# Expert products of a routed mixture: weights loaded in runs of rows, and eight of twelve products a tile as three float32r products each

## Chip, cores and metric

The kernel runs on one core of a Trainium2 chip. The metric is the device time of one execution in microseconds (us). "Before" is the median of three executions.

## What is computed

The program is a whole small model: one mixing block with a hierarchical mixture of experts, then two further layers. Only the mixture matters here. Each of 1024 tokens chooses 2 of 16 experts; an expert is a gated product of width 256.

```
eid = g_idx[:, None] * EXPERTS_PER_GROUP + top_i
gates = jnp.sum(jax.nn.one_hot(eid, N_EXPERTS, dtype=jnp.float32) * weights[..., None], axis=1)
y = jnp.zeros_like(t)                                   # t: 1024 x 1024
for e in range(N_EXPERTS):                              # w_gate, w_up: 1024 x 256, w_down: 256 x 1024
    act = jax.nn.silu(t @ w_gate[e]) * (t @ w_up[e]) * gates[:, e:e + 1]
    y = y + act @ w_down[e]
```

All of it is float32.

## The kernel before

Every engine has its own program, written out by hand; semaphores order them. The mixture is worked in 31 tiles (`MTILES`) of 128 token rows of one expert. Which expert a tile has, its token rows and their weights are tables made on the chip (`et_i`, `tabs`). 2048 rows are filled in, so late tiles are mostly or wholly padding; every tile costs TensorE the same. `experts(eng, step)` (line 583) runs `step(i, o)` for tiles 0 to 2, then a loop of two tiles a turn, then the last four tiles and one step more to drain.

One tile on TensorE, as `expert_pe` (line 1606) orders it:

- `gate_up` (line 1579): the tile's 128 rows stand transposed in `hgT` as eight blocks of 128x128. Each is the stationary operand of one product with 512 columns (256 of w_gate, 256 of w_up), summed in PSUM bank 2 or 3. Eight products, the first five ahead of `turn_act`, three behind it.
- `turn_act` (line 1590): two 128x128 transposes of the previous tile's activations.
- `turn_rows` (line 1571): eight 128x128 transposes of the next tile's gathered rows `hg`.
- `down` (line 1597): the previous tile's two blocks of activations against two halves of w_down: four products of 512 columns.

So a tile has twelve products of 128x128 by 128x512. In float32 each leaves two MATMUL records in the trace. The other engines:

- ScalarE, `expert_act` (line 1133): copies the turned activations out of PSUM (line 1139), the Silu of the gate half (1143), copies the 128x1024 result out of PSUM (1147).
- VectorE, `expert_dve`: gate times up times weight (line 2135), then `rows_to_ht` (line 2122): the turned rows times the norm's gain into `hgT`, two operations of 512 columns (2128).
- SyncE: `load_gu` (line 705) loads w_gate and w_up of tile o+2 once `gate_up` of tile o is done; `load_d` (line 711) loads w_down of tile o+1 once `down` of tile o-1 is done. Weights have two buffers. A partition takes rows p, p+128, ... of a weight matrix, so a run in HBM is one row: 1 KB for gate and up, 4 KB for down.
- GpSimd: `gather` brings the rows of tile o+3, `scatter` writes the result of tile o-1, both as indirect DMAs.

In most of its other large products the kernel already has a split form (`accumulate_split`, line 99): an operand x is kept as hi, a ScalarE copy of x into float32r, and lo = x - hi, a VectorE subtraction; x·w is then hi·hi + hi·lo + lo·hi, three float32r products, each of which leaves one MATMUL record.

Of the kernel before, what the change touches and what calls it, by code (L numbers as in the profile page):

```python
# [46 lines left out]
V_AG, V_FG, V_CB, V_LG, V_LB, V_PB, V_PS, V_QG, V_KG, V_SG, V_CW = 0, 8, 16, 18, 20, 22, 24, 26, 27, 28, 29  # L47
# [63 lines left out]
def program(nc, A, out):  # L111
    ctx = ExitStack()
    with ctx:  # L113
# [6 lines left out]
        def sems(name, n):  # L120
# [42 lines left out]
                    nc.alloc_sbuf_tensor_at("W1c_hi", [P, 2, HALF], F32R, offset=X_at + 4 * 5 * S))  # L163
        lr_rows = nc.alloc_sbuf_tensor_at("LR", [P, S], F32R, offset=WT_at + 4 * S)
# [115 lines left out]
        actT = X[:, M0 + 1024:M0 + 1536].rearrange("p (b k n) -> p b k n", b=2, k=2)  # L280
# [102 lines left out]
        xn_st = sems("xn_st", 2)  # L383
        rw_zero, rw_in, rt_ready, rt_cp, rt_tp = (
# [244 lines left out]
        def _(sp):  # L629
# [75 lines left out]
            def load_gu(i, o):  # L705
                e, p = expert(i, o), o % 2
                wait_past(sp, m_gu, i * 2 + (o - 1))
                sp.dma_start(WT[:, p, :, 0:DE], A["w_gate"][0, ds(e, 1)].rearrange("a (k p) c -> p (a k) c", p=P)).then_inc(m_wgu[p], 16)
                sp.dma_start(WT[:, p, :, DE:2 * DE], A["w_up"][0, ds(e, 1)].rearrange("a (k p) c -> p (a k) c", p=P)).then_inc(m_wgu[p], 16)

            def load_d(i, o):
                e, p = expert(i, o), o % 2
                wait_past(sp, m_dn, i * 2 + (o - 1))
                sp.dma_start(wd[:, p, :, :], A["w_down"][0, ds(e, 1)].rearrange("a (k p) c -> p (a k) c", p=P)).then_inc(m_wd[p], 16)
# [283 lines left out]
        def _(act):  # L998
# [413 lines left out]
        def _(pe):  # L1412
# [158 lines left out]
            def turn_rows(i, o):  # L1571
# [3 lines left out]
                for c in range(KD):  # L1575
                    tp = pe.transpose(bank(c // 4, P, (c % 4) * P), hg[:, p, c * P:(c + 1) * P], ident[:, :])
                tp.then_inc(m_xt, 1)

            def gate_up(i, o, ks):
                p = o % 2  # L1580
                if 0 in ks:
# [833 lines left out]
```

## Time and profile before

| | |
|---|---|
| median of three runs | 2575.41 us (2574.57 to 2576.43) |
| the profiled execution's own time | 2580.86 us |
| its span, first to last instruction | 2579.1 us |
| mean granted TensorE clock | 0.958 of 2.4 GHz |
| busy share: TensorE, VectorE, ScalarE, GpSimd | 91%, 49%, 39%, 18% |
| expert tiles on TensorE | 643.6 to 1002.1 us |
| HBM read, written | 212.13 MB, 41.42 MB |

TensorE's matmul records overlap, since a matmul's end lies behind the start of the next; what a product costs in a stream is the distance between starts, not its duration. All times below are of the profiled execution. It is 0.2% longer than the median of the runs.

### The profile page before, as it was taken

Reading aid. Unit: us, or ns where it says so; the run is one execution under the profiler, and the core shown is the slowest. Engines: PE = TensorE matmul, PEld = TensorE weight load, DVE = VectorE, ACT = ScalarE, POOL = GpSimd, SP = SyncE. Lnnn points to the kernel's source line nnn. Section 1 sums busy time; section 2 is a strip of 40 time slices with the busy share of each in tenths; the row PEclk is TensorE's granted clock in tenths of the full one; section 3 lists DMA queues with packets and bytes.
Section 4 is the critical chain, followed back from the end, with each engine's and each line's share of the span. In section 5 each row is a group of like instructions: output and inputs, shape, how many; then the busy total and the mean of one; then the engine's idle time right before and its main releaser. Section 6 shows DMA issues by size and latency. Waiting matters only on the chain. (4 is left out here: it accounts for less than half of the span.)

```text
span 2579.1 us, 31377 instructions
## 1 busy us (share of the span) xinstructions
PE 2337.2 (91%) x11004; PEld 1758.5 (68%) x11004; DVE 1272.3 (49%) x2049; ACT 1006.3 (39%) x1623; POOL 456.3 (18%) x494
## 2 busy tenths in 40 slices
PE   7999677898999996799999997998899999998996
PEld 5777354684444443677787886887677877886885
DVE  4178777424111113476615776353466426775344
ACT  5222366322111112556453345144566353444233
POOL 1047233210122221311130000000311230000000
PEclk9999889899999997799999999999899999999998
DMA  6200200014899988211110003012111110003021
GB/s 192 94 33 1 93 38 1 9 56 158 282 351 334 328 283 291 95 33 33 34 52 21 11 33 131 33 49 99 35 34 34 33 43 21 11 34 131 33 68 72
DMA packets 207788, 239.71 MB, mean 93 GB/s; under 512 B 45088, under 2 KB 165152, under 8 KB 207648
## 3 DMA queue, kind: packets, MB, share of 16 engines
q1 hardware_dynamic: 197680, 221.06, 25.9%
q0 software_dynamic: 8928, 16.80, 1.8%
q8 instruction: 85, 1.39, 0.2%
q14 instruction: 55, 0.45, 0.1%
q10 hardware_dynamic: 1040, 0.00, 0.0%
HBM read 212.13 MB, written 41.42 MB: 98 GB/s over the span
## 5 line engine op out<-in xcount | busy, mean ns | idle before, releaser
L106 PE MATMUL ps<-WT_lo,HT_hi 128*128 128x512 f32 x832 | 327.5, 394 | 0.0
L107 PE MATMUL ps<-HT_hi,WF_lo 128*128 128x512 f32 x800 | 315.0, 394 | 0.0
L105 PE MATMUL ps<-HT_hi,WU_hi 128*128 128x512 f32 x704 | 285.8, 406 | 18.7 <-DVE H_lo L2169 14.7
L106 PE MATMUL ps<-H_lo,WU_hi 128*128 128x512 f32 x704 | 277.3, 394 | 0.0
L1586 PE MATMUL ps<-WT,MIX 128*128 128x512 f32 x496 | 225.9, 599 | 4.8 <-DVE MIX L2128 4.8
L105 PE MATMUL ps<-W_hi,HT_hi 128*128 128x512 f32 x512 | 204.6, 400 | 8.8 <-DVE MIX_lo L2315 5.9
L107 PE MATMUL ps<-W_hi,MIX_lo 128*128 128x512 f32 x512 | 201.6, 394 | 0.0
L947 POOL TENSOR_TENSOR WF_lo<-WF,WU_hi 128x1024 fp32r<-128x1024 f32 x44 | 115.0, 2614 | 467.8 <-ACT WU_hi L1174 467.8
L106 PEld LDWEIGHTS ps<-WT_lo,HT_hi 128*128 128x128 f32 x832 | 158.8, 191 | 31.8
L107 PEld LDWEIGHTS ps<-HT_hi,WF_lo 128*128 128x128 f32 x800 | 152.4, 191 | 32.9
L105 PEld LDWEIGHTS ps<-HT_hi,WU_hi 128*128 128x128 f32 x704 | 134.3, 191 | 52.0 <-DVE H_lo L2169 15.5
L1586 PEld LDWEIGHTS ps<-WT,MIX 128*128 128x128 f32 x496 | 92.8, 192 | 110.3 <-issue 105.0
L2135 DVE SCALAR_TENSOR_TENSOR X<-X,ps 128x256 f32<-128x256 f32 x31 | 14.9, 481 | 299.8 <-ACT X L1143 299.8
L1349 ACT ACTIVATE xn<-ps,sm 128x1024 f32<-128x1024 f32 x64 | 71.4, 1116 | 222.0 <-DVE sm L2331 222.0
L106 PEld LDWEIGHTS ps<-H_lo,WU_hi 128*128 128x128 f32 x704 | 134.4, 191 | 29.9 <-issue 2.9
L457 POOL TENSOR_SCALAR ss<-ss 128x1 f32<-128x1 f32 x56 | 14.5, 260 | 724.2 <-ACT ps L445 526.0
L445 ACT ACTIVATE ps<-H 128x1024 f32<-128x1024 f32 x40 | 41.1, 1028 | 222.5 <-DVE H L2357 128.6
L464 PE MATMUL ps<-ident,xn 128*128 128x128 f32 x440 | 69.7, 310 | 55.8 <-ACT xn L451 44.7
L105 PEld LDWEIGHTS ps<-W_hi,HT_hi 128*128 128x128 f32 x512 | 97.7, 191 | 29.6 <-DVE MIX_lo L2315 6.3
L95 PE MATMUL ps<-MIX,X 128*128 128x512 f32 x248 | 111.7, 593 | 1.2 <-ACT X L1139 1.2
L107 PEld LDWEIGHTS ps<-W_hi,MIX_lo 128*128 128x128 f32 x512 | 97.6, 191 | 20.9
L464 PEld LDWEIGHTS ps<-ident,xn 128*128 128x128 f32 x440 | 59.3, 160 | 69.2 <-ACT xn L451 50.0
(431 smaller groups left out, 5001.2 us busy)
## 6 DMA issues: line engine op xcount, KB each, us to landing
WT<-in_w_gate SPq DMA_DIRECT2D x31, 1024.0 KB, 5.7
WT<-in_w_up SPq DMA_DIRECT2D x31, 1024.0 KB, 9.2
MIX<-in_w_down SPq DMA_DIRECT2D x31, 1024.0 KB
WF<-in_w_in SPq DMA_DIRECT2D x48, 512.0 KB, 3.8
WT<-in_w_out SPq DMA_DIRECT2D x6, 2048.0 KB, 8.0
H<-in_x SPq DMA_DIRECT2D x16, 512.0 KB, 9.0
h_dram<-H SPq DMA_DIRECT2D x16, 512.0 KB, 3.0
H<-h_dram SPq DMA_DIRECT2D x16, 512.0 KB, 10.7
```

The source lines that it names most:

```text
L95: mm = pe.matmul(o, l, r, start=(i == 0), stop=(i == last))
L105: pe.matmul(o, lh, rh, start=(i == 0), stop=False)
L106: pe.matmul(o, lh, rl, start=False, stop=False)
L107: mm = pe.matmul(o, ll, rh, start=False, stop=(i == last))
L445: act.activation(xn[:, t % 2, :] if squares is None else squares, H[:, t, :], ACT.Square, accum_out=ss[:, t:t + 1]).then_inc(n_ss, 1)
L457: chain.link(pool.tensor_scalar(ss[:, t:t + 1], ss[:, t:t + 1], 1.0 / D, EPS, ALU.mult, ALU.add))
L464: tp = pe.transpose(bank(2 + 2 * (t % 2) + c // 4, P, (c % 4) * P), xn[:, t % 2, c * P:(c + 1) * P], ident[:, :])
L947: pool.tensor_tensor(WFr[:, w, :, 0:n], WF[:, w, :, 0:n], wu_hi[:, w, :, 0:n].bitcast(F32), ALU.subtract).then_inc(ul_ready, 1)
L1349: act.activation(xn[:, g % 2, :], psf[:, (2 + 2 * (g % 2)) * HALF:(4 + 2 * (g % 2)) * HALF], ACT.Exp, scale=MLA_SCALE, bias=sm[:, g % 2, 1 ...
L1586: mm = pe.matmul(bank(2 + p), hgT[:, p, k, :], WT[:, p, k, :], start=(k == 0), stop=(k == KD - 1))
L2135: dve.scalar_tensor_tensor(out=actb[:, o % 2, :], in0=sgb[:, o % 2, :], scalar=tabs_f[:, ds(i * 2 + o, 1), 2:3].rearrange("p a c -> p (a c)"),
```

## The change

It has three parts, all within the experts.

1. Weights in runs of rows. Partition p now takes rows 8p to 8p+7 of w_gate and w_up, and rows 2p, 2p+1 of w_down: 8 KB in one run for each. To match, the transposes take every eighth column of `hg` (`hg_step`) and every second of the activations (`act_step`), and the norm's gain comes in the same order (`V_FR`, one more small load at the start of the program).
2. Eight products as split products: the last four of the eight gate/up products (blocks 4 to 7) and all four of `down`. The first four gate/up products stay float32. The order on TensorE is four, `turn_act`, twelve float32r, `turn_rows`, twelve float32r.
3. Hi parts made on ScalarE, lo parts on VectorE, for every tile: gate and up (2 x 1024 columns), the rows (512), w_down (2 x 1024), the activations (256). The lo part of a weight is written in place. Each hi part has a single buffer, in the region `WF` and in `X`.

The core of the diff:

```diff
+        hgT_hi = nc.alloc_sbuf_tensor_at("XT_hi", [P, 4, P], F32R, offset=X_at + 4 * 7296)
+        act_hi = nc.alloc_sbuf_tensor_at("AT_hi", [P, 2, P], F32R, offset=X_at + 4 * 7808)
+        act_lo = nc.alloc_sbuf_tensor_at("AT_lo", [P, 2, P], F32R, offset=X_at + 4 * 4736)
...
+        wgu = WTf.rearrange("p (b g k c) -> p b g k c", b=2, g=2, k=KD)
+        hg_step = MXf[:, 4096:6144].rearrange("p (b n k) -> p b k n", b=2, k=KD)
+        KS = 4
+        K0 = KD - KS
+        e_hi = wc_hi[1].rearrange("p k n -> p (k n)")
+        wgu_hi = e_hi[:, 0:2 * KS * DE].rearrange("p (g k c) -> p g k c", g=2, k=KS)
+        wd_hi = e_hi[:, 2048:4096].rearrange("p (k n) -> p k n", k=2)
+        act_step = actb.rearrange("p b (n k) -> p b k n", k=2)
...
-                sp.dma_start(WT[:, p, :, 0:DE], A["w_gate"][0, ds(e, 1)].rearrange("a (k p) c -> p (a k) c", p=P)).then_inc(m_wgu[p], 16)
-                sp.dma_start(WT[:, p, :, DE:2 * DE], A["w_up"][0, ds(e, 1)].rearrange("a (k p) c -> p (a k) c", p=P)).then_inc(m_wgu[p], 16)
+                for g, name in enumerate(("w_gate", "w_up")):
+                    sp.dma_start(wgu[:, p, g, :, :], A[name][0, ds(e, 1)].rearrange("a (p k) c -> p (a k) c", p=P)).then_inc(m_wgu[p], 16)
...
+            def gate_up_hi(i, o):
+                p = o % 2
+                act.wait_ge(m_wgu[p], i * 32 + (32 * (o // 2) + 32))
+                for g in range(2):
+                    act.activation(wgu_hi[:, g, :, :], wgu[:, p, g, K0:KD, :], ACT.Copy).then_inc(m_gh, 1)
...
             def expert_act(i, o):
                 t = i * 2 + o
                 if has(i, o - 1):
                     act.wait_ge(m_at, t)
-                    wait_past(act, m_dn, i * 2 + (o - 2))
-                    act.activation(actT[:, p, :, :], quads(4)[:, 0:2, :], ACT.Copy).then_inc(m_aT, 1)
+                    wait_past(act, m_dn, i * 2 + (o - 1))
+                    act.activation(act_hi[:, :, :], quads(4)[:, 0:2, :], ACT.Copy).then_inc(m_aT, 1)
                 if has(i, o):
...
                     act.activation(sgb[:, o % 2, :], bank(2 + o % 2, DE), ACT.Silu).then_inc(m_sg, 1)
+                if has(i, o + 1):
+                    gate_up_hi(i, o + 1)
+                    rows_hi_of(i, o + 1)
                 if has(i, o - 1):
...
                     act.activation(yb[:, p, :], psf[:, 6 * HALF:8 * HALF], ACT.Copy).then_inc(m_y, 1)
+                if has(i, o):
+                    down_hi(i, o)
...
-                    tp = pe.transpose(bank(c // 4, P, (c % 4) * P), hg[:, p, c * P:(c + 1) * P], ident[:, :])
+                    tp = pe.transpose(bank(c // 4, P, (c % 4) * P), hg_step[:, p, c, :], ident[:, :])
...
-                for k in ks:
-                    mm = pe.matmul(bank(2 + p), hgT[:, p, k, :], WT[:, p, k, :], start=(k == 0), stop=(k == KD - 1))
+                    for k in range(K0):
+                        pe.matmul(to, hgT[:, p, k, :], wgu[:, p, :, k, :], start=(k == 0), stop=False)
+                else:
+                    pe.wait_ge(*m_at_tile(m_xl, i, o))
+                    pe.wait_ge(*m_at_tile(m_gl, i, o))
+                    for k in range(KS):
+                        pe.matmul(to, hgT_hi[:, k, :], wgu_hi[:, :, k, :], start=False, stop=False)
+                        pe.matmul(to, hgT_lo[:, p, K0 + k, :], wgu_hi[:, :, k, :], start=False, stop=False)
+                        mm = pe.matmul(to, hgT_hi[:, k, :], wgu_lo[:, p, :, K0 + k, :], start=False, stop=(k == KS - 1))
...
-                pe.wait_ge(m_aT, i * 2 + (o + 1))
-                pe.wait_ge(m_wd[p], i * 16 + (16 * (o // 2) + 16))
+                pe.wait_ge(*m_at_tile(m_al, i, o))
+                pe.wait_ge(*m_at_tile(m_dl, i, o))
...
-                    mm = accumulate(pe, bank(6 + n), [(actT[:, p, k, :], wd[:, p, k, n * HALF:(n + 1) * HALF]) for k in range(2)])
+                    mm = accumulate_split(pe, bank(6 + n), [(act_hi[:, k, :], act_lo[:, k, :], wd_hi[:, k, cs], wd_lo[:, p, k, cs]) for k in range(2)])
...
+            def gate_up_lo(i, o):
+                p = o % 2
+                for g in range(2):
+                    dve.wait_ge(*m_at_tile(m_gh, i, o, 2, g))
+                    ins = dve.tensor_tensor(wgu_lo[:, p, g, K0:KD, :], wgu[:, p, g, K0:KD, :], wgu_hi[:, g, :, :].bitcast(F32), ALU.subtract)
+                ins.then_inc(m_gl, 1)
...
             def expert_dve(i, o):
+                if has(i, o - 1):
+                    dve.wait_ge(m_aT, i * 2 + o)
+                    dve.tensor_tensor(act_lo[:, :, :], quads(4)[:, 0:2, :], act_hi[:, :, :].bitcast(F32), ALU.subtract).then_inc(m_al, 1)
                 if has(i, o):
...
                 if has(i, o + 1):
                     rows_to_ht(i, o + 1)
+                    gate_up_lo(i, o + 1)
+                    rows_lo_of(i, o + 1)
+                if has(i, o):
+                    down_lo(i, o)
```

`rows_hi_of`, `down_hi` on ScalarE and `rows_lo_of`, `down_lo` on VectorE have the same form as the two functions shown.

ScalarE in the loop over the tiles. `WK_hi` holds the hi parts of the weights, `XT_hi` those of the rows, `AT_hi` those of the activations; WT is gate and up, MIX the rows and w_down. Before, one tile:

```order
L1139 ACTIVATE X<-ps 128x256
L1141 REGISTER_ALU
L1143 ACTIVATE X<-ps 128x256
L1147 ACTIVATE X<-ps 128x1024
L589 REGISTER_ALU
L589 COMPARE_AND_BRANCH
```

Now:

```order
L1180 ACTIVATE AT_hi<-ps 128x256
L1184 ACTIVATE X<-ps 128x256
L1163 ACTIVATE WK_hi<-WT 128x1024 x2
L1166 REGISTER_ALU
L1167 ACTIVATE XT_hi<-MIX 128x512
L1192 ACTIVATE X<-ps 128x1024
L1171 REGISTER_ALU
L1173 ACTIVATE WK_hi<-MIX 128x1024 x2
L614 REGISTER_ALU
L614 COMPARE_AND_BRANCH
```

Five operations are new; the hi parts of w_down stand behind the copy of the previous tile's result (L1192), and the copy of the activations (L1180) behind them.

VectorE, the same place. Before, one tile:

```order
L2135 ISA
L2135 SCALAR_TENSOR_TENSOR X<-X,ps 128x256
L2124 REGISTER_ALU
L2128 TENSOR_TENSOR MIX<-ps,vec 128x512 x2
L589 REGISTER_ALU
L589 COMPARE_AND_BRANCH
```

Now, the last tile ahead of the loop:

```order
L2210 TENSOR_TENSOR AT_lo<-ps,AT_hi 128x256
L2214 SCALAR_TENSOR_TENSOR X<-X,ps 128x256
L2186 TENSOR_TENSOR MIX<-ps,vec 128x512 x2
L2193 TENSOR_TENSOR WT_lo<-WT,WK_hi 128x1024 x2
L2198 TENSOR_TENSOR MIX_lo<-MIX,XT_hi 128x512
L2204 TENSOR_TENSOR MIX_lo<-MIX,WK_hi 128x1024 x2
L614 UNCONDITIONAL_BRANCH
```

Six subtractions are new, one ahead of the product of gate and up and five behind the turned rows.

## Rows read from the trace of the kernel before

**Rows 1.** Timeline, TensorE, one tile: start us, us, engine, line, operation, count

```profile
799.70 1.04 PE L1576 MATMUL ps<-ident,MIX 128*128 128x128 f32 x8
800.57 3.60 PE L95 MATMUL ps<-MIX,X 128*128 128x512 f32 x8
804.00 4.46 PE L1586 MATMUL ps<-WT,MIX 128*128 128x512 f32 x10
808.30 0.38 PE L1594 MATMUL ps<-ident,X 128*128 128x128 f32 x2
...
811.09 0.27 PE L1576 MATMUL ps<-ident,MIX 128*128 128x128 f32 x1
```

**Rows 2.** Waits between 680 and 960: waiter, releaser, total us, times, longest

```profile
DVE X L2135 <- ACT X L1143: 242.9, 25, 9.8
```

**Rows 3.** Timeline, TensorE, split products at full clock, first and last of eleven, then of nine

```profile
1299.69 0.39 PE L106 MATMUL ps<-H_lo,WU_hi 128*128 128x512 f32 x1
...
1301.95 0.39 PE L107 MATMUL ps<-HT_hi,WF_lo 128*128 128x512 f32 x1
...
1304.13 0.40 PE L106 MATMUL ps<-H_lo,WU_hi 128*128 128x512 f32 x1
...
1305.98 0.39 PE L105 MATMUL ps<-HT_hi,WU_hi 128*128 128x512 f32 x1
```

**Rows 4.** By line: ns of one (min/median/max), first and last start; strided reads, then plain

```profile
L1555 PE MATMUL ps<-X x2: 411/434/456, 609.0 to 609.3; 128*128 128x128 f32 x2
...
L1556 PE MATMUL ps<-X,ones x2: 412/412/413, 609.5 to 609.8; 128*128 128x128 f32 x2
...
L1576 PEld LDWEIGHTS ps<-ident,MIX x248: 138/140/143, 639.1 to 982.7; 128*128 128x128 f32 x124
L1576 PE MATMUL ps<-ident,MIX x248: 272/273/328, 639.1 to 982.8; 128*128 128x128 f32 x124
...
L1586 PEld LDWEIGHTS ps<-WT,MIX x496: 186/190/338, 643.6 to 992.6; 128*128 128x128 f32 x166
```

**Rows 5.** Groups by form, ScalarE: line, names, form, count, busy us, mean ns of one

```profile
L1174 ACT ACTIVATE WU_hi<-WF 128x1024 fp32r<-128x1024 f32 x44 | 46.4, 1055 | 1.8 <-DMA WF<-in_w_in 1.6
```

**Rows 6.** Groups by form, VectorE: busy us, mean ns of one

```profile
L2310 DVE TENSOR_TENSOR WT_lo<-WT,W_hi 128x512 fp32r<-128x512 f32 x64 | 42.5, 684 | 11.1 <-ACT W_hi L1332 11.1
...
L2315 DVE TENSOR_TENSOR MIX_lo<-MIX,HT_hi 128x1024 fp32r<-128x1024 f32 x32 | 38.8, 1222 | 12.3 <-ACT HT_hi L1337 12.3
...
L2135 DVE SCALAR_TENSOR_TENSOR X<-X,ps 128x256 f32<-128x256 f32 x31 | 14.9, 481 | 299.8 <-ACT X L1143 299.8
```

**Rows 7.** Stretches: us, PE, PEld, DVE, ACT, POOL, clock, DMA share, GB/s

```profile
720.00:800.00 80.00, 80.00 (x242) 39.14 (x241) 11.76 (x21) 12.63 (x22) 17.19 (x28) 1.00 1.00 351
880.00:940.00 60.00, 60.00 (x182) 29.38 (x181) 10.08 (x18) 9.00 (x16) 13.53 (x22) 1.00 0.88 289
1016.00:1026.00 10.00, 3.93 (x16) 3.13 (x16) 8.14 (x10) 5.54 (x9) 3.79 (x5) 0.50 1.02 413
```

**Rows 8.** DMA issues between 720 and 800: count, KB each, us to landing

```profile
WT<-in_w_up SPq DMA_DIRECT2D x7, 1024.0 KB, 9.3
```

**Rows 9.** Timeline, the last tiles, TensorE and ScalarE

```profile
996.87 0.38 PE L1594 MATMUL ps<-ident,X 128*128 128x128 f32 x2
...
997.07 1.02 ACT L1147 ACTIVATE X<-ps 128x1024 f32<-128x1024 f32 x1 [3.05 <-PE ps L95]
...
998.42 3.70 PE L95 MATMUL ps<-MIX,X 128*128 128x512 f32 x8 [1.17 <-ACT X L1139]
```

**Rows 10.** Timeline, TensorE: first expert tile, and split products at half clock

```profile
643.58 1.22 PE L1586 MATMUL ps<-WT,MIX 128*128 128x512 f32 x1 [3.39 <-DVE MIX L2128]
...
483.12 0.63 PE L107 MATMUL ps<-W1a_hi,MIX_lo 128*128 128x512 f32 x1
483.55 0.63 PE L105 MATMUL ps<-W1a_hi,HT_hi 128*128 128x512 f32 x1
```

**Rows 11.** By line: VectorE low parts with and without GpSimd beside them

```profile
L2169 DVE TENSOR_TENSOR H_lo<-MIX,HT_hi x16: 1209/1212/3381, 1046.2 to 1819.4; 128x1024 fp32r<-128x1024 f32 x16
```

More of the change, by code:

```diff
@@ L44 @@
 PLE = 256
-V_AG, V_FG, V_CB, V_LG, V_LB, V_PB, V_PS, V_QG, V_KG, V_SG, V_CW = 0, 8, 16, 18, 20, 22, 24, 26, 27, 28, 29
+V_AG, V_FG, V_CB, V_LG, V_LB, V_PB, V_PS, V_QG, V_KG, V_SG, V_FR, V_CW = 0, 8, 16, 18, 20, 22, 24, 26, 27, 28, 29, 37
 NV1 = V_CW + 2 * TAPS
@@ L279, in program @@
         actb = X[:, M0 + 512:M0 + 1024].rearrange("p (b n) -> p b n", b=2)
-        actT = X[:, M0 + 1024:M0 + 1536].rearrange("p (b k n) -> p b k n", b=2, k=2)
+        assert M0 + 1024 <= 4736 <= M0 + 1280 and M0 + 3584 <= 7296
         yb = X[:, M0 + 1536:M0 + 3584].rearrange("p (b n) -> p b n", b=2)
@@ L644, in _ @@
                             vec(vec1[:, at:at + n], A[name][0].rearrange("(c p) -> p c", p=P))
+                        vec(vec1[:, V_FR:V_FR + 8], A["ffn_norm_g"][0].rearrange("(p c) -> p c", c=KD))
                         vec(kc[:, :], A["kc"])
@@ L713, in load_d @@
                 wait_past(sp, m_dn, i * 2 + (o - 1))
-                sp.dma_start(wd[:, p, :, :], A["w_down"][0, ds(e, 1)].rearrange("a (k p) c -> p (a k) c", p=P)).then_inc(m_wd[p], 16)
+                sp.dma_start(wd[:, p, :, :], A["w_down"][0, ds(e, 1)].rearrange("a (p k) c -> p (a k) c", p=P)).then_inc(m_wd[p], 16)
             def expert_sp(i, o):
@@ L1131, in _, with rows_hi_of, down_hi @@
             act.activation(ang, ang, ACT.Sin).then_inc(rope_set, 1)
+            def gate_up_hi(i, o):
[3 more added lines that the diff above has]
+                    act.activation(wgu_hi[:, g, :, :], wgu[:, p, g, K0:KD, :], ACT.Copy).then_inc(m_gh, 1)
+            def rows_hi_of(i, o):
+                act.wait_ge(m_ht, i * 2 + (o + 1))
+                act.activation(hgT_hi[:, :, :], hgT[:, o % 2, K0:KD, :], ACT.Copy).then_inc(m_xh, 1)
+            def down_hi(i, o):
+                p = o % 2
+                act.wait_ge(m_wd[p], i * 16 + (16 * (o // 2) + 16))
+                for k in range(2):
+                    act.activation(wd_hi[:, k, :], wd[:, p, k, :], ACT.Copy).then_inc(m_dh, 1)
             def expert_act(i, o):
@@ L1580, in gate_up @@
                 p = o % 2
+                to = bank(2 + p).rearrange("p (g c) -> p g c", g=2)
                 if 0 in ks:
@@ L1591, in turn_act @@
                 pe.wait_ge(m_act, i * 2 + (o + 1))
-                wait_past(pe, m_aT, i * 2 + o)
+                pe.wait_ge(*m_at_tile(m_al, i, o - 1))
                 for k in range(2):
-                    tp = pe.transpose(bank(4, P, k * P), actb[:, o % 2, k * P:(k + 1) * P], ident[:, :])
+                    tp = pe.transpose(bank(4, P, k * P), act_step[:, o % 2, k, :], ident[:, :])
                 tp.then_inc(m_at, 1)
@@ L1607, in expert_pe @@
                 if has(i, o):
-                    gate_up(i, o, range(0, 5))
+                    gate_up(i, o, range(0, K0))
                 if has(i, o - 1):
@@ L1611, in expert_pe @@
                 if has(i, o):
-                    gate_up(i, o, range(5, KD))
+                    gate_up(i, o, range(K0, KD))
                 if has(i, o + 1):
```

33 lines of the change are left out of this document (28 added, 5 removed).

## The prediction

> **What bounds the kernel now.** I read the timeline of TensorE for one tile in the middle of the experts first. The reader should see a closed chain: the eight transposes of turned rows start at 799.70 and the next tile's at 811.09, so a tile takes 11.39 us, and each group starts before the one ahead of it ends [rows 1]. Eight records of float32 products fill 800.57 to 804.00, or 0.429 us from start to start. Twelve products are 24 records, 10.29 us; ten transposes are the rest. Second, the waits of that stretch: the longest are VectorE's for ScalarE, 242.9 us in 25 waits, and that is an engine with nothing to do, since TensorE has no wait in the list [rows 2]. Third, the same stretch in one line: TensorE busy 80.00 of 80 us at a granted clock of 1.00 (2.4 GHz), VectorE 11.76, ScalarE 12.63, and the DMA engines at a share of 1.00 with 351 GB/s [rows 7]. So TensorE sets the pace, 31 tiles long, and the DMA engines stand right behind it.
>
> **What the change takes away.** A float32 product is two records, 0.857 us. Float32r records elsewhere in the program follow each other after 0.226 us (ten steps from 1299.69 to 1301.95) or 0.231 us (eight steps from 1304.13 to 1305.98) [rows 3]. I take 0.229, so three of them are 0.687 us, and a split product saves 0.170 us. Eight a tile save 1.36 us, and 31 tiles save 42.2 us (40.7 to 44.3 with either end). Four float32 products, the order of the groups and the number of transposes stay.
>
> **The transposes with a stride.** The turned rows are now read at every eighth column, 32 bytes apart. In a transpose the data is the stationary operand (the record names the moving one, `ident`, first), so the stride falls on the weight load. No row shows a strided weight load. The nearest rows are two products whose moving operand of 128 columns has just this stride: 412 ns each, where a transpose with a plain moving operand of 128 columns takes 273 [rows 4]. That is 139 ns more. A float32 record of 512 columns takes 429 ns, so one of 128 takes 107, and I read each as two runs through the columns, 54 ns a run: 139 ns is then 69 ns for one run. The weight load of a float32 product takes 190 ns and that of a transpose 140 [rows 4]; the 50 ns between them are about one run, so I take it that a transpose loads its data in a single one. That run grows from 54 to 123 ns and lies beside the identity's 107 ns of the transpose before. What sticks out is 16 ns, or 0.13 us for eight and 4.0 us for 31 tiles. Lower bound: 0. Upper bound: the longest strided record, 456 ns [rows 4], would add 0.18 us to each transpose. The activations are read at every second column; their two transposes I cost at nothing, and with the same 16 ns they would cost under 1 us in all.
> The Trainium skill (SBUF — State Buffer, Door 1) says that reads keep full bandwidth only while at least two accesses in a row fall into the same 16-byte line, so every eighth float32 pays and every second does not. The strided moving operands agree with it; whether a weight load pays the same is open, and by that rule alone the sum could not say how much.
>
> **The new work on ScalarE and VectorE.** ScalarE: a hi part of 1024 columns is 1.055 us [rows 5]; four of them and one of half that size add 4.8 us. With the copy of the result, 1.02 [rows 9], and two operations of 256 columns (at most VectorE's 0.48 for that shape), it comes to some 6.7 us a tile. VectorE: 1.222 us for 1024 columns, 0.684 for 512, 0.481 for 256, and 2 x 0.684 for the turned rows, which have the shape of the 512-column row [rows 6]: 4 x 1.22 + 0.68 + 0.48 + 1.37 + 0.48 = 7.9 us. Both lie below the new period of 11.39 - 1.36 + 0.13 = 10.16 us, but each waits in order, so I walk through a tile, with zero at the end of `gate_up(o)`. TensorE: `turn_rows(o+1)` to 1.0, `down(o-1)` to 3.7, float32 part of `gate_up(o+1)` to 7.2, `turn_act(o)` to 7.4, split part to 10.1. ScalarE: Silu to 0.6, gate and up hi to 2.8, rows hi to 3.4, then it waits for `down(o-1)`, result to 5.0, w_down hi to 7.1, activations hi at 7.6. VectorE: product to 1.2, turned rows to 2.6, gate and up lo to 5.0, rows lo to 5.7, w_down lo to 8.5, activations lo to 9.0. TensorE wants the rows at 3.7 (there at 2.6), the split operands at 7.4 (5.7) and those of `down(o)` at 11.1 (9.0). The smallest slack is 1.1 us, so this work costs nothing in the middle. The cover is those slacks; past them every late microsecond is one of the tile.
>
> **The weights' DMAs.** The bytes stay. A tile moves 351 GB/s x 11.39 us = 4.00 MB; in 10.16 us that is 394 GB/s, at engines whose share is already 1.00. But those are 1 KB runs in two of three matrices. With 4 KB rows alone the same engines move 413 GB/s over 10 us [rows 7], and now every run is 8 KB. So the demand is 95% of a rate seen, and I cost it at nothing, on thin cover. Landing: w_up lands 9.3 us after its issue [rows 8], near 9.8 after the end of `gate_up`. TensorE asked for it 4.5 us after the next such end; now ScalarE asks at 0.6, which leaves about 1 us even at the old landing time, and the chain behind has 1.7 us more.
> The Trainium skill (DMA: Bandwidth & Descriptors, Bandwidth) puts the HBM share of a core at about 358 GB/s and says that this side binds; by it a full tile would take 11.2 us and most of the gain would be lost. The 413 GB/s measured here with one core at work contradict it, and the measurement decides.
>
> **Start and end.** The first float32 product starts at 643.58 after 3.39 us without work, at 1.2 GHz [rows 10]. Its operands come as before; the hi and lo parts of tile 0 (5.5 us of ScalarE and VectorE in turn, less what overlaps) are done by about 647, and the split part is reached only at 650. Cost nothing. The end does cost. Now the last `down` starts at 998.42, 1.55 us after `down` of the tile before has ended at 996.87 [rows 9]. In the change the single hi buffer of w_down, and its place behind the copy of the result, put in a row after that end: wait 0.2, result 1.02, two hi parts 2.1, second lo part and its wait 1.3, activations lo 0.5: start at 5.1 us, so 3.6 later. After such a pause the clock is at 1.2 GHz, as at 643.58, where split records are 0.43 us apart (483.12 to 483.55) [rows 10]: twelve take 5.2 us and not 2.75, 2.4 more. Together 6.0 us.
> The load of `V_FR` is one of nineteen small ones at the start; at most a few tenths, taken as nothing.
>
> **The sum.** -42.2 + 4.0 + 6.0 = -32.2 us. The profiled execution, 2580.9, would become 2548.7; the median of the runs is 5.5 us below it, so the median becomes 2575.4 - 32.2 = **2543.2 us**. Some 0.2% (5 us) is what a measurement of this kernel can tell from no change.
>
> **Rivals.**
> 1. *Strided weight loads are dear.* If a transpose costs c more, the time is 2575.4 - 42.2 + 6.0 + 248 c = 2539.2 + 248 c. It breaks even at c = 0.146 us. With 0.139, the price of the strided records in full, it is 2574 (same); with 0.183, the longest of them, it is 2585, **slower** than before. For it: the only strided float32 reads in the trace are that dear [rows 4]. Against it: the moving operand runs twice and the stationary one once, under cover. This would be so if the weight load were not hidden. Chance 0.13, split between same and slower.
> 2. *The DMA engines become the bound.* If the rate stays 351 GB/s whatever the runs, a full tile takes 11.4 us and not 10.16. Late tiles are padding: between 880 and 940 the rate is 289 GB/s [rows 7], 3.29 MB a tile, which even at 351 takes 9.4 us. With an estimated 14 full tiles at 1.23 us and seven half-way ones at 0.6 the loss is 22 us: 2565. At 380 GB/s a full tile loses 0.37, in all 5 us: 2548. For it: share 1.00. Against it: 413 GB/s. Chance 0.13.
> 3. *VectorE and GpSimd keep each other out.* One subtraction of the same kind and shape took 3381 ns, the others 1209 [rows 11]; it ran beside a GpSimd operation on SBUF. In a tile GpSimd is busy 17.2 us in 80, 2.4 us a tile [rows 7], mostly in issuing indirect DMAs. If all of it were added, VectorE would be at 10.3 us, some 0.2 us over the period, and waits in order would add more: with 0.5 us a tile, 15 us lost, 2558. Chance 0.07; a stall of over 1 us a tile, which gives all back, 0.04 more.
>
> **Numbers.** My forecast has 0.63. Faster by over 0.2%: forecast, rivals 2 and 3, 0.83. Same: 0.09 (rival 1 at 0.139, part of 3). Slower: 0.08 (rival 1 at 0.183, a stall of over 1 us). The range: below, no price for the stride, 0.226 us a record and an end of 4 us, 2575.4 - 44.3 + 4 = 2535; above, rival 2 in full, 2565, which also takes in a stride price of 0.10 us. I give 2534 to 2566.
>
> **What would show it.** In the profile after: a tile of 10.1 us in TensorE's timeline without a wait in the middle; float32r records 0.23 us apart; eight transposes in 1.0 us in place of 0.87 (1.9 or more would be rival 1); a DMA share of 0.95 and about 390 GB/s with waits for `WT` loads absent (rival 2: ScalarE waiting for the DMA and a tile of over 10.5 us); VectorE busy 7.9 us a tile; one wait of about 5 us ahead of the last `down`, with the clock at half behind it. I am wrong if TensorE waits for VectorE's lo parts in every tile.

## The result

| | before | after |
|---|---|---|
| median of 4 runs each | 2575.38 us (2574.57 to 2576.43) | 2538.80 us (2534.18 to 2540.82) |
| ratio, 95% interval | | 0.9858 (0.9846 to 0.9871) |
| profiled execution, span | 2580.86, 2579.1 us | 2540.82, 2539.0 us |
| mean granted clock | 0.958 | 0.959 |
| busy share: TensorE, VectorE, ScalarE, GpSimd | 91%, 49%, 39%, 18% | 90%, 57%, 45%, 19% |
| one tile on TensorE (mean of 29 steps) | 11.397 us | 10.047 us |
| experts: first product to the start of the last result copy | 358.58 us | 322.60 us |

The change is 36.6 us faster; 32.2 were forecast, and 2538.80 lies in the range. The two profiled executions differ by 40.0 us, of which the experts give 35.98. Of the rest, 1.7 us lie ahead of the experts' first product (643.58 and 641.85) and 2.3 behind the experts, in stages that the change doesn't touch. So experiments are compared below by the last row of the table too: from the timeline, the start of the first float32 product of `gate_up` to the start of ScalarE's last 128x1024 copy. It has a part that no change here meant to move: the clock is at half when the experts start, and the first eight float32 records took 5.93 us in the change, 5.56 in e4 and 4.83 in e3. A difference of 1 us between two stages therefore says little unless the tiles or the end show it too.

In the lines of the profile PE is TensorE, PEld its weight loads, DVE VectorE, ACT ScalarE, POOL GpSimd and SPq the DMA queue of SyncE. First the timeline of TensorE for one tile after the change [rows 1, 3]. Of the runs of split records only the first two of `down` and the first of gate and up stand here.

```profile
800.55 1.04 PE L1626 MATMUL ps<-ident,MIX 128*128 128x128 f32 x8
801.35 0.48 PE L105 MATMUL ps<-WK_hi,AT_hi 128*128 128x512 f32 x1
801.67 0.39 PE L106 MATMUL ps<-MIX_lo,AT_hi 128*128 128x512 f32 x1
...
804.19 3.59 PE L1637 MATMUL ps<-WT,MIX 128*128 128x512 f32 x8
807.62 0.39 PE L1651 MATMUL ps<-ident,X 128*128 128x128 f32 x2
807.76 0.47 PE L1642 MATMUL ps<-WK_hi,XT_hi 128*128 128x512 f32 x1
...
810.60 1.04 PE L1626 MATMUL ps<-ident,MIX 128*128 128x128 f32 x8
```

The eight transposes now take 0.80 us to the next group, `down` 2.84 (twelve records, 801.35 to 804.19), the four float32 products 3.43, the two transposes 0.14 and the split part 2.84. That is 10.05 us, a closed chain again: each group starts before the one ahead ends. Split records start 0.23 us apart, as [rows 3]. The periods between one tile's activation transposes and the next's are 10.04 or 10.05 us, 29 times out of 29.

Stretches, in the columns of [rows 7]:

```profile
720.00:800.00 80.00, 80.00 (x336) 56.86 (x335) 58.66 (x72) 49.12 (x64) 24.56 (x32) 1.00 1.00 392
880.00:940.00 60.00, 60.00 (x252) 42.65 (x251) 43.60 (x54) 37.08 (x48) 16.57 (x22) 1.00 0.84 323
```

TensorE is still busy all the time at a clock of 1.00. VectorE does 7.4 us a tile (58.66 / 80 x 10.05) and ScalarE 6.2. The DMA engines' share is 1.00 as it was, but they now move 392 GB/s where the same share moved 351.

Waits between 660 and 940, in the columns of [rows 2]:

```profile
DVE X L2214 <- ACT X L1184: 57.5, 28, 2.6
...
ACT WK_hi L1163 <- DMA WT<-in_w_up: 15.2, 16, 1.8
```

VectorE's 242.9 us of waiting for the Silu [rows 2] are down to 57.5, since it has work. ScalarE waits for w_up in 16 tiles, up to 1.8 us. No wait of TensorE's matmuls stands in the list.

Groups by form between 680 and 940, ScalarE and VectorE: line, names, form, count, busy us, mean ns of one, idle time before [rows 5, 6].

```profile
L2193 DVE TENSOR_TENSOR WT_lo<-WT,WK_hi 128x1024 fp32r<-128x1024 f32 x52 | 61.2, 1218 | 5.1 <-ACT WK_hi L1163 4.9
L1163 ACT ACTIVATE WK_hi<-WT 128x1024 fp32r<-128x1024 f32 x52 | 52.1, 1052 | 15.3 <-DMA WT<-in_w_up 15.2
...
L2198 DVE TENSOR_TENSOR MIX_lo<-MIX,XT_hi 128x512 fp32r<-128x512 f32 x26 | 17.8, 683 | 0.0
L1167 ACT ACTIVATE XT_hi<-MIX 128x512 fp32r<-128x512 f32 x26 | 16.1, 620 | 0.5 <-issue 0.3
...
L2210 DVE TENSOR_TENSOR AT_lo<-ps,AT_hi 128x256 fp32r<-128x256 f32 x26 | 10.8, 414 | 0.0
...
L1180 ACT ACTIVATE AT_hi<-ps 128x256 fp32r<-128x256 f32 x26 | 10.0, 384 | 13.6 <-PE ps L1651 13.5
```

Each form costs what [rows 5, 6] gave for it; the two operations on activations were taken at 0.48 at most and cost 0.38 and 0.41. Landing times of the loads between 720 and 800 [rows 8]:

```profile
WT<-in_w_gate SPq DMA_DIRECT2D x8, 1024.0 KB, 7.7
WT<-in_w_up SPq DMA_DIRECT2D x8, 1024.0 KB, 11.1
```

w_up lands 11.1 us after its issue instead of 9.3. The start of the stage [rows 10]:

```profile
641.85 6.50 PE L1637 MATMUL ps<-WT,MIX 128*128 128x512 f32 x8 [3.32 <-DVE MIX L2186]
647.78 0.79 PE L1642 MATMUL ps<-WK_hi,XT_hi 128*128 128x512 f32 x1
```

The split part of the first tile starts as soon as the float32 part ends. And the end [rows 9], TensorE, ScalarE and VectorE:

```profile
953.97 0.39 PE L1651 MATMUL ps<-ident,X 128*128 128x128 f32 x2
954.17 1.02 ACT L1192 ACTIVATE X<-ps 128x1024 f32<-128x1024 f32 x1 [2.34 <-PE ps L107]
955.09 1.99 ACT L1173 ACTIVATE WK_hi<-MIX 128x1024 fp32r<-128x1024 f32 x2
...
956.17 2.36 DVE L2204 TENSOR_TENSOR MIX_lo<-MIX,WK_hi 128x1024 fp32r<-128x1024 f32 x2 [3.83 <-ACT WK_hi L1173]
956.98 0.38 ACT L1180 ACTIVATE AT_hi<-ps 128x256 fp32r<-128x256 f32 x1
...
958.45 0.42 DVE L2210 TENSOR_TENSOR AT_lo<-ps,AT_hi 128x256 fp32r<-128x256 f32 x1
...
958.92 0.79 PE L105 MATMUL ps<-WK_hi,AT_hi 128*128 128x512 f32 x1 [4.56 <-DVE AT_lo L2210]
...
959.51 0.63 PE L106 MATMUL ps<-MIX_lo,AT_hi 128*128 128x512 f32 x1
...
964.45 1.02 ACT L1192 ACTIVATE X<-ps 128x1024 f32<-128x1024 f32 x1 [7.08 <-PE ps L107]
```

From the last activation transposes to the last `down` there are now 4.95 us and not 1.55, with the chain that was forecast: result copy, two hi parts, lo parts, activations lo. The products after it are 0.43 us apart, at half clock (1.2 GHz).

### The profile page after: what moved, and what is told of

Its sections match the earlier page's. It is cut to its first block and busy times, and to the rows that moved or that the text cites. A ratio compares the mean times of both kernels' runs of the same rounds, so it can differ in the third digit from the quotient of the medians.

```text
span 2539.0 us, 32489 instructions
## 1 busy us (share of the span) xinstructions
PE 2296.5 (90%) x11252; PEld 1807.1 (71%) x11252; DVE 1444.4 (57%) x2235; ACT 1142.5 (45%) x1778; POOL 477.3 (19%) x494
## 5 line engine op out<-in xcount | busy, mean ns | idle before, releaser
L1637 PE MATMUL ps<-WT,MIX 128*128 128x512 f32 x248 | 114.4, 605 | 4.7 <-DVE MIX L2186 4.7
L1965 DVE SCALAR_TENSOR_TENSOR H<-H,vec 128x1024 f32<-128x1024 f32 x60 | 89.0, 1525 | 0.5
L1637 PEld LDWEIGHTS ps<-WT,MIX 128*128 128x128 f32 x248 | 47.8, 194 | 53.6 <-issue 46.2
L2204 DVE TENSOR_TENSOR MIX_lo<-MIX,WK_hi 128x1024 fp32r<-128x1024 f32 x62 | 73.3, 1222 | 18.6 <-ACT WK_hi L1173 18.6
## 6 DMA issues: line engine op xcount, KB each, us to landing
H<-h_dram SPq DMA_DIRECT2D x16, 512.0 KB, 11.1
```

The costliest lines, as they stand in the source:

```text
L1637: pe.matmul(to, hgT[:, p, k, :], wgu[:, p, :, k, :], start=(k == 0), stop=False)
L1965: o = dve.scalar_tensor_tensor(out=y_cv[:, c, :], in0=uu, scalar=w, in1=y_cv[:, c, :], op0=ALU.mult, op1=ALU.add)
L2204: ins = dve.tensor_tensor(wd_lo[:, p, k, :], wd[:, p, k, :], wd_hi[:, k, :].bitcast(F32), ALU.subtract)
```

## The experiments

All ratios are against the kernel before, run on the same chip in the same batch. There were four batches (the change; e1 to e4; e5 to e8; e9 and e10), and the median of before was 2575.38, 2574.75, 2576.48 and 2574.45 us in them, so medians of two batches are compared only roughly. "Stage" is the experts' measure defined above. "Tile" is the mean of 29 steps; where a few steps stand out (e5, e6, e9) it is that of the others, and e2 has the range.

| kernel | median us | ratio (95% interval) | tile us | stage us |
|---|---|---|---|---|
| before | 2575.38 | | 11.397 | 358.58 |
| the change | 2538.80 | 0.9858 (0.9846 to 0.9871) | 10.047 | 322.60 |
| e1, runs of rows alone | 2574.22 | 1.0003 (0.9992 to 1.0014) | 11.42 | 358.92 |
| e2, split products, short runs | 2546.65 | 0.9903 (0.9886 to 0.9920) | 10.02 to 11.32 | 330.05 |
| e3, plain transposes | 2536.09 | 0.9862 (0.9846 to 0.9879) | 10.028 | 320.93 |
| e4, two hi buffers of w_down | 2531.74 | 0.9840 (0.9823 to 0.9856) | 10.05 | 316.86 |
| e5, five of eight split | 2533.48 | 0.9831 (0.9812 to 0.9851) | 9.88, nine steps more | 316.30 |
| e6, six of eight split | 2564.05 | 0.9955 (0.9941 to 0.9969) | 10.96, first step 13.59 | 347.03 |
| e7, gate and up alone split | 2553.54 | 0.9915 (0.9894 to 0.9936) | 10.75 | 337.49 |
| e8, down alone split | 2562.06 | 0.9940 (0.9919 to 0.9961) | 10.73 | 343.73 |
| e9, e5 with a semaphore for w_gate | 2530.53 | 0.9825 (0.9811 to 0.9838) | 9.88, two steps more | 312.78 |
| e10, e4 with the same | 2533.56 | 0.9843 (0.9829 to 0.9858) | 10.05 | 316.10 |

### The first part of the change alone (e1)

The loads take eight (two) rows in a run, transposes read with the stride and the gains come from `V_FR`; every product stays float32:

```
...
-    mm = pe.matmul(bank(2 + p), hgT[:, p, k, :], WT[:, p, k, :], start=(k == 0), stop=(k == KD - 1))
+    mm = pe.matmul(bank(2 + p).rearrange("p (g c) -> p g c", g=2), hgT[:, p, k, :], wgu[:, p, :, k, :], start=(k == 0), stop=(k == KD - 1))
```

> The kernel before with part 1 alone: 8 KB runs, strided transposes, all twelve products in float32. My theory (TensorE sets the pace, transfers and the stride are hidden): a tile stays at 11.39 to 11.42 us, the transposes' weight loads take 188 ns in place of 140, the DMA share falls from 1.00 to about 0.87 between 720 and 800, the time is 2575 +- 2 us. Rival (the longer runs brought part of the gain, since the DMA engines held TensorE back): a tile under 11.3 us and 2565 us or less.

It took 2574.22 us, ratio 1.0003, tile 11.42. Its stretch, to be set beside [rows 7]:

```profile
720.00:800.00 80.00, 80.00 (x240) 39.86 (x239) 11.76 (x21) 12.54 (x21) 17.23 (x29) 1.00 0.93 345
```

The runs of rows bring no time by themselves: at the old pace the loads were never late. The stride costs 0.023 us a tile (11.420 against 11.397). The DMA engines move 345 GB/s, nearly as much, at a share of 0.93 and not 1.00 (about 0.87 was expected).

### The first part undone (e2)

Split products as in the change, but the weights in 1 KB and 4 KB runs and transposes of adjacent columns:

```
-    sp.dma_start(wgu[:, p, g, :, :], A[name][0, ds(e, 1)].rearrange("a (p k) c -> p (a k) c", p=P))
+    sp.dma_start(wgu[:, p, g, :, :], A[name][0, ds(e, 1)].rearrange("a (k p) c -> p (a k) c", p=P))
...
-    tp = pe.transpose(bank(c // 4, P, (c % 4) * P), hg_step[:, p, c, :], ident[:, :])
+    tp = pe.transpose(bank(c // 4, P, (c % 4) * P), hg[:, p, c * P:(c + 1) * P], ident[:, :])
...
```

> The changed kernel with part 1 undone: split products, but weights in 1 KB and 4 KB runs and plain transposes. My theory (1 KB runs hold the DMA engines at about 351 GB/s): full tiles take 11.4 us in place of 10.05, with waits of ScalarE for the loads of WT, in all some 22 us more, 2561 us. Rival (the share of 1.00 is no limit, TensorE sets the pace with either run length): 10.05 us a tile and 2537 to 2541 us.

Its stretches, its waits between 680 and 940, and the landing of w_up:

```profile
720.00:800.00 80.00, 77.67 (x323) 53.62 (x322) 55.68 (x70) 44.71 (x61) 20.53 (x32) 1.00 1.04 368
800.00:880.00 80.00, 79.05 (x328) 54.27 (x327) 56.97 (x71) 46.28 (x62) 20.68 (x30) 1.00 1.04 363
...
ACT WK_hi L1163 <- DMA WT<-in_w_up: 52.8, 21, 4.1
...
DVE WT_lo L2193 <- ACT WK_hi L1163: 35.8, 20, 3.3
...
WT<-in_w_up SPq DMA_DIRECT2D x8, 1024.0 KB, 13.3
```

Full tiles take up to 11.3 us, most of them 10.4 to 11.2, and padded ones 10.02, so neither the expectation (11.4 us in every full tile, 2561 us) nor its rival (10.05 us) was met. The short runs cost 7.5 us of the stage and 7.9 of the medians (9.1 of the stage beside e3 below, which has the same transposes), well under half of the 22 that rival 2 of the prediction gave. With the very runs of before the engines move 368 GB/s (373 between 680 and 720), so the 351 of [rows 7] was what the kernel asked for and no limit, though the share stood at 1.00 there. At 368 the loads are late: w_up lands after 13.3 us, ScalarE waits for it 21 times and VectorE behind it. So the long runs are what lets the split products pay in full, while alone they pay nothing.

### Transposes without the stride (e3)

The kernel loads and computes as the change does, but the transposes take adjacent columns, so that rows and weights no longer belong together: it computes other sums.

```
-    tp = pe.transpose(bank(c // 4, P, (c % 4) * P), hg_step[:, p, c, :], ident[:, :])
+    tp = pe.transpose(bank(c // 4, P, (c % 4) * P), hg[:, p, c * P:(c + 1) * P], ident[:, :])
...
```

> The changed kernel with contiguous reads in the ten transposes of a tile, the loads in long runs kept. It changes which row meets which weight, so it computes other sums of the same size. My theory (the stride is hidden under the identity's two runs): weight loads of 140 ns again, a tile of 10.03 to 10.05 us, 2538 +- 2 us. Rival (the stride costs 16 ns a transpose, as the prediction had it): a tile of 9.92 us and 2534.5 us.

By line, in the columns of [rows 4]: the change first, then e3.

```profile
L1626 PEld LDWEIGHTS ps<-ident,MIX x248: 185/188/208, 637.4 to 941.9; 128*128 128x128 f32 x124
...
L1651 PEld LDWEIGHTS ps<-ident,X x62: 195/197/200, 656.5 to 954.0; 128*128 128x128 f32 x62
```

```profile
L1626 PEld LDWEIGHTS ps<-ident,MIX x248: 138/140/142, 638.4 to 941.2; 128*128 128x128 f32 x124
...
L1651 PEld LDWEIGHTS ps<-ident,X x62: 138/140/143, 656.4 to 953.3; 128*128 128x128 f32 x62
```

A weight load with the stride of 32 bytes takes 188 ns and not 140, but the tile only 10.047 and not 10.028 us: 0.019 us, 0.6 us over 31 tiles. One of e3's 29 steps took 10.25 us; without it the mean is 10.020, and the stride costs 0.027 us a tile or 0.8 us in all. (The other 1.1 us of the stage's 1.67 lie in the first tile, in the first eight float32 records.) So of 48 ns more some 2 or 3 stick out. A load's record is longer than what it holds up: in the change's timeline the eight strided loads of a tile fill 800.32 to 801.40, 1.08 us for eight records of 0.188, which are 1.50 us in sum, so the records overlap one another.

### Two hi buffers of w_down (e4)

This takes away what makes the last `down` late. The hi parts of w_down go to two buffers in turn, and ScalarE makes them ahead of the copy of the result:

```
-    act.activation(wd_hi[:, k, :], wd[:, p, k, :], ACT.Copy).then_inc(m_dh, 1)
+    act.activation(wd_hi2[p][:, k, :], wd[:, p, k, :], ACT.Copy).then_inc(m_dh, 1)
...
+                if has(i, o):
+                    wait_past(act, m_dn, i * 2 + (o - 1))
+                    down_hi(i, o)
                 if has(i, o - 1):
```

> The changed kernel with a second buffer for the hi parts of w_down and these hi parts ahead of the copy of the result on ScalarE. My theory (the end costs what the single buffer puts in a row): the last down starts 2.1 us after the one before it and not 4.95, at full clock, its records 0.23 us apart and not 0.43, together 5.2 us less: 2533.6 us, a tile still 10.05 us. Rival (ScalarE copies the result 1.4 us later in every tile, which holds up down or the activations): a tile of 10.2 us or more and no gain in all, 2538 us or more.

Its end, TensorE and ScalarE:

```profile
951.12 0.39 PE L1654 MATMUL ps<-ident,X 128*128 128x128 f32 x2
951.32 1.02 ACT L1197 ACTIVATE X<-ps 128x1024 f32<-128x1024 f32 x1 [0.45 <-PE ps L107]
952.24 0.38 ACT L1182 ACTIVATE AT_hi<-ps 128x256 fp32r<-128x256 f32 x1
...
953.13 0.50 PE L105 MATMUL ps<-WK_hi,AT_hi 128*128 128x512 f32 x1 [1.62 <-DVE AT_lo L2213]
...
956.20 1.02 ACT L1197 ACTIVATE X<-ps 128x1024 f32<-128x1024 f32 x1 [3.58 <-PE ps L107]
```

The last `down` starts 2.01 us after the transposes, at full clock, and the last copy follows 3.07 us later instead of 5.53. From 951.12 to the last copy's start at 956.20 is 5.08 us, against 10.48 in the change (953.97 to 964.45). That is 5.4 us less; the tile is the same. The medians differ by 7.1 over two batches, and in the profiled executions the stage also started 2.5 us earlier (639.34 against 641.85); what the end gives is the 5.4.

### The two halves of the split (e7, e8)

e7 keeps float32 in `down`, e8 in `gate_up`; each drops the hi and lo parts that only the other half needs.

```
e7:
-    mm = accumulate_split(pe, bank(6 + n), [(act_hi[:, k, :], act_lo[:, k, :], wd_hi[:, k, cs], wd_lo[:, p, k, cs]) for k in range(2)])
+    mm = accumulate(pe, bank(6 + n), [(actT[:, p, k, :], wd[:, p, k, n * HALF:(n + 1) * HALF]) for k in range(2)])
e8:
-    for k in range(KS):
-        pe.matmul(to, hgT_hi[:, k, :], wgu_hi[:, :, k, :], start=False, stop=False)
-        pe.matmul(to, hgT_lo[:, p, K0 + k, :], wgu_hi[:, :, k, :], start=False, stop=False)
-        mm = pe.matmul(to, hgT_hi[:, k, :], wgu_lo[:, p, :, K0 + k, :], start=False, stop=(k == KS - 1))
+    for k in range(K0, KD):
+        mm = pe.matmul(to, hgT[:, p, k, :], wgu[:, p, :, k, :], start=False, stop=(k == KD - 1))
```

> Runs of rows for all weights, and only the four gate/up products of a tile split; the two products of down (four pairs of 512 columns) stay float32, and what served them (hi parts of w_down and of the activations, their lo parts) is gone. My theory (the gain is the count of records on TensorE, the last pause is that of the split down): four products of 512 columns save 4 x 0.170 = 0.68 us a tile, so 11.397 - 0.68 + 0.026 = 10.74 us a tile, 31 tiles save 20.4 us, and the last down starts some 1.6 us after the one before it at the full clock, as before the change: 2575.0 - 20.4 = about 2554.6 us. Rival (the gain comes from the longer runs once TensorE leaves room, or from a wait that only the pair of both removes): then the two halves do not add, and the tile is over 10.9 us, 2559 or more.

> Runs of rows for all weights, and only the four products of down of a tile split; the four gate/up products stay float32, without hi and lo parts of w_gate, w_up and the turned rows. My theory: a tile of 11.397 - 0.68 + 0.026 = 10.74 us as in the other half, but with the pause ahead of the last down of 4.9 us instead of 1.55 and its twelve records 0.43 us apart, +6 us: 2575.0 - 20.4 + 6 = about 2560.6 us, some 6 us over the kernel with gate/up alone split. Rival (the pause at the end is only partly the split down, since ScalarE and VectorE have less work ahead of it here): 2555 to 2558.

2553.54 and 2562.06 us, within 1.5 us of both sums. Tiles of 10.75 and 10.73 us: each half gives half, and the two save 22.9 and 14.4 us, together 37.4 where the whole change saves 36.6; of the stage they save 21.1 and 14.9, together 35.9, where the whole saves 36.0. The stages differ by 6.2 us, which is the end: e7's last `down` starts 1.55 us after the transposes (973.10 to 974.65), e8's 4.94. Its rows also show the clock falling:

```profile
975.29 0.39 PE L1642 MATMUL ps<-ident,X 128*128 128x128 f32 x2
...
980.23 0.51 PE L105 MATMUL ps<-WK_hi,AT_hi 128*128 128x512 f32 x1 [4.55 <-DVE AT_lo L2201]
...
980.57 0.60 PE L106 MATMUL ps<-MIX_lo,AT_hi 128*128 128x512 f32 x1
...
980.97 0.63 PE L107 MATMUL ps<-WK_hi,AT_lo 128*128 128x512 f32 x1
...
983.96 0.42 PE L105 MATMUL ps<-WK_hi,AT_hi 128*128 128x512 f32 x1
...
984.22 0.40 PE L106 MATMUL ps<-MIX_lo,AT_hi 128*128 128x512 f32 x1
```

After the pause of 4.55 us the first steps are 0.34 and 0.40 us, then 0.43 until 983.96, then 0.23 to 0.26 again. The rival, a shorter pause where the engines have less ahead of it, is out: the chain is the same in length with half the work.

### More products split (e5, e6)

Both have e4's buffers; `KS` is 5 and 6 instead of 4.

> As the changed kernel, but five instead of four of the eight gate/up products split, with two hi buffers of w_down and the hi parts of w_down ahead of the copy of the result, as in the kernel with two buffers. My theory (TensorE's record count still sets the pace): 10.05 - 0.17 = 9.88 us a tile, 5 us less in all: 2531.7 - 5.1 = 2526.6 us; full tiles would then move 4.00 MB in 9.88 us, 405 GB/s. Rival 1 (DMA engines at their end at the share of 1.00 and 392 GB/s): a full tile stays at 10.0 to 10.2 us and the time at 2529 to 2534. Rival 2 (VectorE's order): the split part is wanted 6.4 us into a tile, and the gate/up and rows lo parts are ready at about 6.2; half a microsecond later there each tile costs 15 us: 2540.

> As the one before with six of the eight gate/up products split. If only the count of TensorE's records mattered, 9.71 us a tile and about 2521 us. My theory: two float32 products remain ahead of the split part, which is then wanted 5.5 us into a tile, while VectorE (product, turned rows, six lo parts of gate and up, rows lo in order) has its operands at about 6.9; TensorE waits some 1.4 us for VectorE's lo parts in every tile, the tile is about 11.1 us and the time about 2564: slower than with four.

e6 took 2564.05 us, as forecast, though its count of records would give 2521. Stretch and TensorE's wait between 660 and 930:

```profile
720.00:800.00 80.00, 73.17 (x320) 55.23 (x320) 62.72 (x66) 51.98 (x60) 30.49 (x30) 1.00 0.92 361
...
PE ps L1645 <- DVE MIX_lo L2201: 23.7, 24, 1.3
```

TensorE waits about 1 us in each tile where 1.4 were forecast, and the tile is 10.96 us and not 11.1. That the total fits all the same is partly luck: the first step took 13.59 us, since a wait of 2.00 us in it was followed by eight steps at half clock. VectorE has 8.6 us of work in a tile (62.72 / 80 x 10.96). It isn't VectorE's rate that binds, but its place: the operands of a split part that comes earlier in the tile are made in the tile.

e5 missed by 7 us, and its stage is only 0.6 us below e4's. Twenty of its 29 steps take 9.87 or 9.88 us as forecast (the expectation of e9, written before, counts 21), four take 9.93 or 9.94 and five 10.5 to 11.2. One of these five, ScalarE, VectorE and TensorE:

```profile
781.17 2.43 ACT L1165 ACTIVATE GU_hi<-WT 128x1280 fp32r<-128x1280 f32 x2 [1.41 <-DMA WT<-in_w_up]
...
783.51 0.72 ACT L1169 ACTIVATE XT_hi<-MIX 128x640 fp32r<-128x640 f32 x1
...
785.29 0.82 DVE L2201 TENSOR_TENSOR MIX_lo<-MIX,XT_hi 128x640 fp32r<-128x640 f32 x1
...
786.16 0.50 PE L1645 MATMUL ps<-GU_hi,XT_hi 128*128 128x512 f32 x1 [0.39 <-DVE MIX_lo L2201]
```

ScalarE's hi parts start only at 781.17, released by w_up's landing; VectorE's last lo part starts at 785.29, and TensorE, which had come to the split part at 785.5, starts it at 786.16. So VectorE's order (rival 2) and a late load act together: the load is late in some tiles by what four split products could take and five can't. The time lies within rival 1's 2529 to 2534 us, but that alone doesn't show that the DMA engines were at their end; e9 asks this.

### A semaphore of its own for w_gate (e9, e10)

To tell lateness from a lack of bandwidth, ScalarE now starts on w_gate when it has landed, before w_up has. Two signals that order on VectorE makes needless were dropped for the semaphores.

```
-    sp.dma_start(wgu[:, p, g, :, :], ...).then_inc(m_wgu[p], 16)
+    sp.dma_start(wgu[:, p, g, :, :], ...).then_inc((m_wga, m_wgu)[g][p], 16)
...
-                act.wait_ge(m_wgu[p], i * 32 + (32 * (o // 2) + 32))
                 for g in range(2):
+                    act.wait_ge((m_wga, m_wgu)[g][p], i * 16 + (((WGA0[p], 0)[g]) + 16 * (o // 2) + 16))
```

> The kernel with five of eight split, with one thing changed: the loads of w_gate and w_up count on semaphores of their own, so that ScalarE rounds w_gate's columns to hi parts as soon as w_gate has landed, while w_up is still on its way. In the kernel with one semaphore 21 of 29 tiles took 9.88 us and eight took 0.05 to 1.3 us more, the late ones after ScalarE had waited for w_up. My theory (w_up lands late, and ScalarE and VectorE then do two hi and two lo parts and the rows' in a row): one hi part of 1.2 us less stands behind the landing, VectorE's lo parts come up to 1.2 us earlier, most of the slow tiles go to 9.88 us and 3 to 5 us are saved: 2533.5 - 4 = about 2529.5 us. Rival (the slow tiles are a lack of bandwidth, 4.00 MB in 9.88 us being 405 GB/s): the delay only moves, the sum of the tiles is the same and the time stays at 2533.

> The same change of semaphores in the kernel with two hi buffers for w_down and four of eight split, where TensorE waited in no tile though ScalarE waited for w_up as long. My theory: every tile stays at 10.05 us and nothing changes, 2531.7 us; e9, with five split, is then the fastest of all by some 2 us. Rival (the early hi part helps the pace of the loads themselves): under 2530.

e9's stretch, and ScalarE's waits for w_down and w_up between 660 and 930:

```profile
720.00:800.00 80.00, 80.00 (x351) 59.47 (x350) 64.36 (x74) 54.02 (x66) 26.14 (x32) 1.00 1.00 398
...
ACT WK_hi L1176 <- DMA MIX<-in_w_down: 16.0, 16, 1.8
ACT GU_hi L1166 <- DMA WT<-in_w_up: 5.4, 8, 0.8
```

The tiles that were late are gone: 27 of 29 steps at 9.88 us; the first, 10.6 in both, is the one that stays. The same loads move 398 GB/s where e5 moved 390, so bandwidth was there, and 3.5 us of stage are saved where 4 were expected. (The medians, of two batches, differ by 3.0 us, the ratios by 0.0006 with intervals that overlap, so the tiles are the evidence.) The rival was right in one thing: part of the delay did move. ScalarE waits for w_up 5.4 us and not 12.8, but for w_down 16.0 and not 1.9, and no matmul waits between 660 and 930. e10 stays at 10.05 us a tile and, from its first activation transposes to the last copy, at 302.14 us against e4's 302.16: nothing, as expected. Its median is 1.8 us above e4's, measured in another batch. In one batch e9 is 3.0 us below e10, and its slowest execution is faster than e10's fastest. e9 is the fastest kernel of this study, 1.75% below before.

## Why the prediction was right

- **What bounds the kernel.** TensorE's records, right. Every kernel without a wait of TensorE's follows their count: 11.397, 10.75, 10.73, 10.047, 9.88 us for no, four, four, eight and nine split products.
- **What the change takes away.** -42.2 us forecast. The period fell by 1.350 us, which over 31 tiles is -41.8 with the stride in it. With the stride's 0.02 to 0.03 added back, a split product saves 0.171 or 0.172 us, against 0.170.
- **The transposes with a stride.** This term was mis-sized, and it is nearly all of the forecast's error: +4.0 us forecast, 0.6 to 0.8 measured (e3; e1 gives 0.7). The step that failed is "what sticks out is 16 ns". The weight load grew by 48 ns and not by 69, and then about 3 ns of it stuck out per transpose (0.019 to 0.027 us over eight). The growth was what I had wrong, a price taken from moving operands: with 48 in its place the same reckoning gives 54 + 48 = 102 ns beside the identity's 107, and nothing sticks out. The sign given for the term, eight transposes in 1.0 us in place of 0.87, did not come either: they took 0.80. Whether the strided records of [rows 4] are two runs of the moving operand was not tested. Rival 1 is out: c is about 0.003 us, and it breaks even at 0.146.
- **ScalarE and VectorE.** Forecast 6.7 and 7.9 us a tile, measured 6.2 and 7.4. In a row of two equal operations the second starts before the first one's record ends (two hi parts of 1.05 us take 1.99). No tile waited for them. Rival 3 is out: with GpSimd busy 24.6 of 80 us, the lo parts of 1024 columns stayed at 1.22 us, and the longest of the 124 took 1.30.
- **The weights' DMAs.** Forecast 394 GB/s, measured 392, with no wait of TensorE's. But "on thin cover" was right as well: w_up lands 11.1 us after its issue, and ScalarE waits for it in 16 tiles, up to 1.8 us, which VectorE's slack still covers. e5 shows what happens when that slack goes. Rival 2 took the 351 GB/s for a limit; e2 shows 368 to 373 with those same runs.
- **Start and end.** Start: nothing, right. End: +6.0 forecast. The last `down` starts 4.95 us after the transposes and not 1.55: +3.4 (3.6 forecast). From there to the last copy are 5.53 us, where e4 at full clock took 3.07: +2.5 (2.4 forecast). e4 shows both terms by taking them away, e8 by leaving them where only `down` is split.

The sum with the measured terms: 31 tiles, -41.8 with the stride; end +5.9; together -35.9, against -35.98 for the stage and -36.6 between the medians. Of the forecast's error of 4.4 us the stride is 3.2 to 3.4; the rest is less than the medians can tell. The 31 tiles and the end came out as forecast, by the mechanism that was forecast.

The Trainium skill (DMA: Bandwidth & Descriptors, Bandwidth), weighed in the prediction, puts a core's share of the HBM at about 358 GB/s. This case goes past it for 160 us on end in the change (392, then 372 between 800 and 880), and e9 moves 398, with one core at work. The same section gives that share for two cores that stream at once and has 425 GB/s measured with one alone, which the prediction left out; the rates here lie between the two, and no run here has two cores at work.

## What to carry to other kernels

Where a matmul engine is the bound, count its records per product, and price the preparation by where it falls in the tile, not by its busy share: six split products were slower than four because their operands came 1 us late in each tile, with VectorE idle for a fifth of the time. A change to the loads that does nothing alone can be what lets another change pay: compare the pair with each half undone. And a DMA share of 1.00 doesn't say that the engines can't move more; look whether anyone waits for the landing.

## What the runs showed of the hardware

- A transpose's weight load grew from 140 to 188 ns with a stride of 32 bytes, and to 197 ns with one of 8 bytes (the rows of L1626 and L1651 above). The Trainium skill (SBUF — State Buffer, Door 1) says that full bandwidth needs at least two accesses in a row to one 16-byte line; by that rule every second float32 would be free and every eighth would pay. In these weight loads both pay, and the smaller stride not less.
- The same share of 1.00 stood beside 351 GB/s and 392. With short runs it is 0.28 per 100 GB/s (before, and e2 with 1.04 at 368), with long ones 0.27 and 0.26 (e1 with 0.93 at 345, and the change), all between 720 and 800.
- After a pause of 4.56 us TensorE's clock was at half for all of the last `down` (the change); after 4.55 in e8 two steps were faster before it stood at half; after 1.62 in e4 it stayed at full. In e6 pauses of 1.38 us (to 653.01) and 2.00 us (to 657.22) in the first tile were followed by eight steps of 0.43 to 0.46 us, while its later waits of about 1 us a tile cost no clock: it is 1.00 between 720 and 800.
